# Recurrence of a bidirectional gated DeltaNet: the interleaved projection units 2, 0, 2, 0, 2, 0 over steps 2 to 7 in place of 1 in each

## What is computed

```python
h = rmsnorm(x, norm_w) * (1 + scale) + shift
proj = h @ w_in                      # q, k, v, z_a, x_b, z_b, gate columns
# branch A, 8 heads of 128, both directions, chunks, per head and direction:
def step(s, xs):
    w_c, u_c, qg_c, qk_c, kd_c, dl_c = xs
    v_new = u_c - w_c @ s            # needs the state of the step before
    o_c = qg_c @ s + qk_c @ v_new
    s = s * dl_c + kd_c.T @ v_new    # the next state
    return s, o_c
# branch B: RG-LRU; then merge by sigmoid gates, output projection, residual, final rmsnorm
```

## Time and profile before

| | |
|---|---|
| median of 3 runs | 1489.98 us (1489.16 to 1490.83) |
| the profiled execution, its own time | 1488.63 us |
| its span (first to last instruction) | 1486.8 us |
| TensorE matmuls, busy | 1471.0 us, 99% |
| VectorE busy | 1016.0 us, 68% |
| ScalarE busy | 798.6 us, 54% |
| GpSimd busy | 350.5 us, 24% |
| mean granted TensorE clock | 0.998 |
| share of the chain that ended last | TensorE 96% |

### The profile page before, as it was taken

One profiled execution on the slowest core, in us unless ns is written; L12 is line 12 of the kernel. 1 busy time (PEld: TensorE's weight loads), 2 busy tenths in 40 slices (PEclk: granted clock), 3 DMA queues, 4 the chain that ended last, 5 costly groups with the idle time before them and its releaser, 6 DMA issues.

```text
span 1486.8 us, 28072 instructions
## 1 busy us (share of the span) xinstructions
PE 1471.0 (99%) x11376; PEld 1414.2 (95%) x11376; DVE 1016.0 (68%) x1815; ACT 798.6 (54%) x1645; POOL 350.5 (24%) x296
## 2 busy tenths in 40 slices
PE   8999999999999999999999999999999999999997
PEld 7899999999999999999899999999999999999886
DVE  5799897988889898888847744744836611534254
ACT  6574857566584857566476564574576500322111
POOL 2122322232232322132211221221221211342110
PEclk9999999999999999999999999999999999999999
DMA  9322121122213112222311221211212531543132
GB/s 316 116 69 92 33 73 55 45 80 63 79 33 110 31 52 79 88 79 83 120 52 46 82 63 48 82 55 56 82 52 90 180 113 43 174 140 105 42 127 99
DMA packets 122435, 127.46 MB, mean 86 GB/s; under 512 B 6745, under 2 KB 105922, under 8 KB 122306
## 3 DMA queue, kind: packets, MB, share of 16 engines
q1 hardware_dynamic: 122018, 125.34, 26.9%
q10 hardware_dynamic: 288, 0.33, 0.1%
HBM read 105.56 MB, written 20.09 MB: 85 GB/s over the span
## 4 chain that ended last, share of the span: by engine, by line
PE 96%; DVE 1%; SPq 1%; DMA 1%; issue 1%; ACT 0%; POOLq 0%; POOL 0%; DVEq 0%
PE mb L134 16%; PE mb L135 16%; PE mb L136 16%; PE db L134 10%; PE db L136 9%; PE db L135 9%; PE db L1374 3%; PE db L1346 2%; PE db L1390 2%; PE db L1363 2%; PE db L1384 2%; PE db L1008 2%; PE db L1315 1%; PE db L1233 1%; PE db L1194 1%; PE db L1298 1%
## 5 line engine op out<-in xcount | busy, mean ns | idle before, releaser
L134 PE MATMUL mb<-h_hi,w_hi 128*128 128x384 f32 x1080 | 363.0, 336 | 0.0
L135 PE MATMUL mb<-h_lo,w_hi 128*128 128x384 f32 x1080 | 362.9, 336 | 0.0
L136 PE MATMUL mb<-h_hi,w_lo 128*128 128x384 f32 x1080 | 362.9, 336 | 0.0
L134 PE MATMUL db<-h_hi,w_hi 128*128 128x384 f32 x816 | 287.9, 353 | 0.2 <-DVE w_lo L1472 0.2
L136 PE MATMUL db<-h_hi,w_lo 128*128 128x384 f32 x816 | 274.6, 336 | 0.0
L135 PE MATMUL db<-h_lo,w_hi 128*128 128x384 f32 x816 | 274.5, 336 | 0.0
L2074 POOL TENSOR_TENSOR w_lo<-w,w_hi 128x1024 fp32r<-128x1024 f32 x47 | 127.2, 2708 | 459.5 <-ACT w_hi L2109 459.5
L134 PEld LDWEIGHTS mb<-h_hi,w_hi 128*128 128x128 f32 x1080 | 203.0, 188 | 0.1
L136 PEld LDWEIGHTS mb<-h_hi,w_lo 128*128 128x128 f32 x1080 | 203.0, 188 | 0.0
L135 PEld LDWEIGHTS mb<-h_lo,w_hi 128*128 128x128 f32 x1080 | 203.0, 188 | 0.0
L134 PEld LDWEIGHTS db<-h_hi,w_hi 128*128 128x128 f32 x816 | 153.7, 188 | 4.1 <-DVE w_lo L1472 0.7
(11 more groups left out here) (339 smaller groups left out, 2908.5 us busy)
## 6 DMA issues: line engine op xcount, KB each, us to landing
w<-in_w_in SPq DMA_DIRECT2D x48, 512.0 KB, 4.0
d_dt<-decay_rows SPq DMA_DIRECT2D x16, 576.0 KB, 6.5
d_qg<-decay_rows SPq DMA_DIRECT2D x16, 512.0 KB, 4.2
w<-in_w_gate SPq DMA_DIRECT2D x16, 512.0 KB, 4.2
branch_a<-d_kq SPq DMA_DIRECT2D x8, 576.0 KB, 3.3
branch_b<-l_z SPq DMA_DIRECT2D x8, 576.0 KB, 2.8
merge_gates_b<-l_gates SPq DMA_DIRECT2D x8, 576.0 KB, 5.5
m_in<-merge_gates_b SPq DMA_DIRECT2D x8, 576.0 KB
```

The source lines that it names most:

```text
L134: pe.matmul(out, hi, rhi, start=(k == 0), stop=False)
L135: pe.matmul(out, hi, rlo, start=False, stop=False)
L136: return pe.matmul(out, lo, rhi, start=False, stop=(last and stop))
```

## The change

Step 2, 4 and 6 of the recurrence take two units each, steps 3, 5 and 7 none; steps 0, 1 and 8 keep 2, 2 and 1. It holds for heads 0 to 6. The sum is 24 before and after, and the order of the units is the same.

```diff
                 lru_shares = (1, 1, 1, 1, 1, 1, 1, 1, 0)
-                shares = (15, 2, 3, 3, 1) if last else (4, 2, 2, 3, 2, 2, 2, 1, 1, 1, 1, 1, 1, 1)
+                shares = (15, 2, 3, 3, 1) if last else (4, 2, 2, 3, 2, 2, 2, 2, 0, 2, 0, 2, 0, 1)
```

## The result

| | before | after |
|---|---|---|
| median | 1490.4 us (1489.16 to 1490.95, 4 runs) | 1499.93 us (1499.08 to 1501.13, 4 runs) |
| span of the profiled execution | 1486.8 us | 1499.3 us |
| mean granted clock | 0.998 | 0.999 |

The ratio is 1.0068, with a 95% interval of 1.0056 to 1.0080: 9.5 us slower by the medians, 8.3 to 11.9 by the interval. Forecast were 10.3 us more and 1500.3 us.

A forecast was written before the change was run, and what follows sets the result against it. The prediction took the loop of tap, `vnu`, p2, `vk`, p3, new state as the bound, not TensorE; 21 pairs x 0.49 = 10.3 us on 1488.63 gave 1498.9, plus 1.35 to the median: 1500.3 us, range 1497.2 to 1502.0.

The forecast's parts named there:

- The loop bounds the step, not TensorE's stream: Recurrence steps 2 to 7: tap, `vnu`, p2, `vk`, p3, new state close a 2.91 us loop without the unit.
- Step with two units, 3.40: Steps 2, 4, 6: first unit hidden, second costs 0.53; 1.54 to p2 plus 1.86 makes 3.40 us.
- the bound of 3.44: Upper bound in us for a two-unit step, taken from step 1 of the kernel before.
- Step without, 2.91, not 2.80: Steps 3, 5, 7: stay at 2.91 us; 2.80 kept for the range; rival of 0.11 less, 1498.0 us, chance 0.06.
- One unit is free: In a recurrence step, one unit lies beside the loop between p1 and p2; its absence saves nothing.
- The 0.08 that the prediction read as p2's wait: In a one-unit step p2 takes 0.52 us, against 0.44 in step 1; 0.08 is an unlisted wait.
- Sum, 21 x 0.49 = 10.3: Three pairs of steps in seven heads, each 6.31 in place of 5.82 us: 10.3 us more.
- Everything outside as before: Outside the recurrence nothing changes; each head's recurrence is longer by 1.5 us.
- Given back between recurrences: Rival: other engines use the longer recurrences, TensorE wins at most 4.2 us of listed waits; 1496.1 us, chance 0.04.
- faster by TensorE's stream: Rival: units on the path, empty steps take 2.30 us; 2.5 us gained, 1487.5 us, chance 0.03.
- The clock: Forecast: clock unaffected. Rival: idling brings 1.2 GHz from step 3 to 8, 109 us more, some 1609 us, chance 0.02.

The follow-up runs named there:

- five other kernels with full-size taps: Kernel before with other unit shares: one pair alone; pairs mirrored; three units ahead of the recurrence; three units in steps 2 and 5; six in step 2. 1492.68 to 1509.62 us.
- small taps: Taps of heads 1 to 7 treat one column, against the kernel before: 1486.84 us; the same with the change's shares: 1495.55 us.
- split taps: Against the kernel before, each tap of steps 1 to 7 cut in halves, one behind `vnu`, one behind `vk`: 1499.74 us, ratio 1.0071.
- all seven of those profiles: Profiles of the kernel before (1490.4 us), the changed one (1499.93 us) and the five with other shares and full taps (1492.68 to 1509.62 us).
- the execution of 1609.89 us: One execution of the kernel before with steps 2, 4, 6 empty and 3, 5, 7 doubled (otherwise 1500.81 us); clock 0.85, no trace, left out of ratios.
- split taps with pairs: Tap halves behind `vnu` and `vk`, plus the change's shares, against the kernel before: 1514.23 us, 25.0 us more.

## Why the prediction was right

- **The loop bounds the step, not TensorE's stream.** Right. Empty steps took 2.90 to 2.92 in the change and in five other kernels with full-size taps where they were, at whatever place and with up to five on end.
- **Step with two units, 3.40.** Right, 3.38 to 3.41; the bound of 3.44 wasn't needed. The second unit's 0.53 and the 1.86 from p2 on were both found again (1.85 in the step shown).
- **Step without, 2.91, not 2.80.** Right, and the reason too: with the tap made small it was 2.80. The last head's step 8 could be read for this step because what differed there, the missing tap, was known.
- **"One unit is free".** Right in this kernel, but a little too wide as I then used it. The small taps showed that it is free because the tap holds `vnu` back: without the tap the one-unit step takes 2.87 and only the empty one 2.80. The 0.08 that the prediction read as p2's wait was gone then (p2 took 0.44), but p3 took 0.52 to the next product in place of 0.49, so TensorE's own 2.77 isn't reached. My expectations for the small and the split taps missed by that 0.07 per step.
- **Sum, 21 x 0.49 = 10.3.** The steps of the profile gave 7 x 1.44 = 10.1 and the medians 9.5. "Everything outside as before" was not quite so in the profiled pair: 2.4 us more lay in step 1 of two heads and outside the recurrences. The forecast had no term for the first: a long step 1 depends on whether GpSimd's select starts ahead of VectorE's two taps, and that differs from profile to profile: head 4 has it in all seven of those profiles, heads 0, 2 and 5 in some. The interval of the medians, 8.3 to 11.9 us, holds 10.3 with and without these 1.3 us, so the time alone doesn't show that the forecast lacked them.
- **Given back between recurrences; faster by TensorE's stream.** Neither happened. Taking the units out to the stretch between recurrences costs there just what they cost as second units.
- **The clock.** It stayed in the change, but the rival is no phantom: with one more idle of 1.46 us close by, it fell, in four heads of seven. The margin was not known when the forecast gave it 0.02, and these runs place it only roughly. Whether the execution of 1609.89 us was this rival stays open: the time is the rival's 1609, but its 42 steps of 2.91 + 2.6 us at 0.50 would leave a mean clock of some 0.93 (an estimate), not 0.85. "TensorE: Matmul & The Clock Gate" of the Trainium skill, in the section named in the prediction, speaks of short and frequent idling as enough to make the clock swing between its levels (the rival had it stay low for six steps); by that rule, the trace of five empty steps on end does not agree (1.00), and that of the split taps with pairs does (0.50), if a wait of 1.46 us is called short.

## What to carry to other kernels

Before fillers are moved in a loop that several engines share, add up the starts around the loop without the filler: if that sum is the step, the slot is free up to its own length and lost when left empty, and a doubled slot pays in full. A TensorE at 99% busy can still be waiting in every step; distances between starts show it, the list of waits doesn't. When VectorE work is moved to a gap, look at what GpSimd does in that gap, not only at whether the length fits.

## What the runs showed of the hardware that was not expected

- A VectorE instruction with two tensors in SBUF (128x193) took 2.22 to 2.23 us in place of 0.41 while GpSimd's tensor_tensor of 2.36 us ran, in all seven heads of the split taps, and those with a PSUM operand kept their 0.61 (kernel before, head 1). Beside affine_select, when it had started first, two taps of 128x386 took 2.41 to 2.94 us in place of 1.14.
- The granted clock of TensorE was at 0.50 for over 2 us after a wait of 1.46 us in a step without a unit, in four heads of seven (split taps with pairs). It stayed at 1.00 over five such steps on end with a listed idle of 0.3 us each (six units in step 2), and after a wait of 1.42 to 1.44 us in a step with a unit (split taps).
